# Three-pass products in place of plain ones, a convolution product cut into pieces among attention units, and masks computed one block ahead

## The reference

```python
# block 1: projection, then three mixers whose outputs are joined and projected
cb, cc, cx, nq, nk, nv, gqkv, gz, ga, gb = jnp.split(hmix @ w_in[l], split_at, axis=-1)
y_conv = cb * _dwconv(cc * cx, conv_a_w[l])
y_na   = _neighbourhood_attention(...)          # 4 heads, bias added to the scores
y_gdn  = _gdn_mixer(...)                        # chunked gated delta rule, both directions
# inside it: lower = (kb @ k.T) * dec_strict ; a unit lower triangular solve per chunk of 64
#            intra = (q @ k.T) * dec_incl
...
# then y = concat(y_conv, y_na, y_gdn) @ w_out, and a mixture of 32 experts, 2 of them per token
```

## Time and profile before

| what | value |
|---|---|
| median of 3 runs | 3724.31 us |
| the profiled execution, its own time | 3726.51 us |
| its span from first to last instruction | 3724.6 us |
| PE busy | 3312.6 us, 89% of the span |
| DVE busy | 1811.9 us, 49% |
| ACT busy | 1243.9 us, 33% |
| granted TensorE clock, mean | 0.926 of full |
| share of the chain that ended last | PE 83%, DVE 8%, ACT 4%, issue 3%, DMA 1% |

### The profile page before, as it was taken

How to read it: one execution, slowest core, us unless ns; L and a number is a source line. 1 busy time by engine, 2 the same in 40 slices (tenths; PEclk the granted TensorE clock), 3 DMA queues, 4 the chain that set the end, 5 groups by cost and what they waited for, 6 DMA issues and landing times.

```text
span 3724.6 us, 34562 instructions
## 1 busy us (share of the span) xinstructions
PE 3312.6 (89%) x13568; PEld 2320.0 (62%) x13568; DVE 1811.9 (49%) x2689; ACT 1243.9 (33%) x1864; POOL 44.4 (1%) x76
## 2 busy tenths in 40 slices
PE   7987678789999976899899899999799978969997
PEld 3644676467667653658664378877577755438786
DVE  5335554256566544513562145554598855133343
ACT  2215113255555533215242122222422254032233
POOL 0000000000000000000000000000000000000000
PEclk9998889889999997999899999999899966989999
DMA  8420001379999962212013125541122210103220
GB/s 287 153 96 1 1 1 65 140 293 385 384 379 390 376 252 101 91 68 91 23 46 113 62 76 190 189 151 62 43 79 88 91 68 1 68 23 113 79 79 23
DMA packets 146798, 486.12 MB, mean 131 GB/s; under 512 B 8176, under 2 KB 11888, under 8 KB 134128
## 3 DMA queue, kind: packets, MB, share of 16 engines
q1 hardware_dynamic: 130544, 438.58, 31.6%
q10 hardware_dynamic: 10368, 24.79, 1.7%
q0 software_dynamic: 5760, 20.97, 1.4%
HBM read 459.15 MB, written 25.17 MB: 130 GB/s over the span
## 4 chain that ended last, share of the span: by engine, by line
PE 83%; DVE 8%; ACT 4%; issue 3%; DMA 1%; SPq 0%; POOL 0%; POOLq 0%; ACTq 0%; DVEq 0%; PEldq 0%
PE bank L456 15%; PE bank L458 14%; PE bank L457 14%; PE bank L355 14%; PE bank L1603 5%; PE bank L1114 3%; PE bank L2182 2%; PE bank L553 2%; PE bank L2766 2%; PE bank L545 1%; PE bank L2788 1%; PE bank L1571 1%; DMA ring<-in_w_ada 1%; PE bank L2776 1%; PE bank L2626 0%
## 5 line engine op out<-in xcount | busy, mean ns | idle before, releaser
L457 PE MATMUL bank<-h_parts,A_parts 128*128 128x512 f32 x1424 | 561.3, 394 | 0.0
L355 PE MATMUL bank<-A,ring 128*128 128x512 f32 x800 | 350.0, 600 | 15.1 <-DVE A L1260 8.4
L456 PE MATMUL bank<-h_parts,A_parts 128*128 128x512 f32 x816 | 323.4, 396 | 35.9 <-DVE h_parts L2984 13.4
L458 PE MATMUL bank<-h_parts,ring_parts 128*128 128x512 f32 x848 | 333.8, 394 | 0.0
L445 ACT ACTIVATE A_parts<-ring 128x1024 fp32r<-128x1024 f32 x162 | 170.4, 1053 | 420.9 <-PE bank L458 420.1
L457 PEld LDWEIGHTS bank<-h_parts,A_parts 128*128 128x128 f32 x1424 | 271.7, 191 | 58.6 <-issue 3.8
L452 DVE TENSOR_TENSOR ring_parts<-ring,A_parts 128x1024 fp32r<-128x1024 f32 x162 | 198.0, 1223 | 205.4 <-ACT A_parts L445 205.4
L355 PEld LDWEIGHTS bank<-A,ring 128*128 128x128 f32 x800 | 153.9, 193 | 209.4 <-issue 193.0
L1642 DVE TENSOR_TENSOR ring_parts<-ring,h_parts 128x1024 fp32r<-128x1024 f32 x192 | 225.7, 1221 | 42.7 <-ACT h_parts L1705 41.9
L458 PE MATMUL bank<-h_parts,A_parts 128*128 128x512 f32 x576 | 227.6, 395 | 0.0
L456 PE MATMUL bank<-A_parts 128*128 128x512 f32 x544 | 214.8, 395 | 5.3 <-DVE A_parts L2492 5.2
(11 more groups left out here) (493 smaller groups left out, 5398.5 us busy)
## 6 DMA issues: line engine op xcount, KB each, us to landing
ring<-in_expert_w SPq DMA_DIRECT2D x64, 2048.0 KB, 9.3
ring<-in_w_in SPq DMA_DIRECT2D x37, 2048.0 KB, 7.9
A<-in_expert_w SPq DMA_DIRECT2D x32, 2048.0 KB, 9.4
ring<-in_w_ada SPq DMA_DIRECT2D x24, 2048.0 KB, 12.4
ring<-in_w_ff SPq DMA_DIRECT2D x16, 2048.0 KB, 7.6
slot_rows<-A ACTq DMA_DIRECT2D x32, 512.0 KB, 9.2
ring<-in_w_ffn_gate SPq DMA_DIRECT2D x5, 2048.0 KB, 7.7
ring<-in_w_ffn_up SPq DMA_DIRECT2D x5, 2048.0 KB, 7.9
```

Of the source, the lines that this page charges most:

```text
L355: mm = pe.matmul(bank[tile % 4][:], ring_tile(g)[:, k, m * P:(m + 1) * P], rhs(k), start=(k == 0), stop=(k == g.kt - 1))
L456: pe.matmul(out, parts(w_high), parts(r_low), start=start, stop=False)
L457: pe.matmul(out, parts(w_high), parts(r_high), start=False, stop=False)
L458: return pe.matmul(out, parts(w_low), parts(r_high), start=False, stop=stop)
```

## The change

- Five products go from `project` to `project_split`: `out`, `wa2`, `wb2`, `wo2`, `wo3`. Their activations are parted too: `high_of` (a copy on ACT, 128 by 512) and `low_of` (a subtraction on DVE).
- `co3`, the convolution's output product, also becomes three-pass, and is cut into 32 pieces of two weight squares (6 matmuls) that stand in loops 5 to 22 of the attention: one ahead of `turn(u)`, a second behind it. All pieces write bank 1, so `turn` keeps bank 0 alone. `back` stands one loop later, and so does the DVE step `to_gates` behind it. The sum of the two branches, formerly per tile behind `co3`, is done by column blocks inside the attention and at its end.
- The masks of block b+1 are cut into stages that stand between the steps of block b's inverse. Two constant squares are joined into four, which leaves 9 DVE operations per direction instead of 10.
- `bias_dve` moves ahead into the input projection. Neighbourhood attention no longer waits for `ada11` at its start.
- The bias row in block 2 is added by PE (a matmul of one row per square) instead of DVE.
- Ring slots of block 3: `co3` and `wo3` use slots 0 and 1, the first `ff1` granules slots 2 and 3, whose loads wait for the end of `wo3`. All five first expert loads wait for the end of `out`, formerly two were issued ahead of it.

```diff
@@ in_dve, na_pe
             gdn_decays_dve(dve)
+            bias_dve(dve)
...
-            pe.wait_ge(sem("tile_read"), L["ada11"][0].first_tile + 1)
+            pe.wait_ge(sem("tile_read"), L["xq_in"][0].first_tile + 4)
@@ block1_pe (the same way on ACT and DVE)
+            mask_rows_pe(pe, 0)
+            mask_dots_pe(pe, 0, 0)
+            mask_dots_pe(pe, 0, 1)
             for b in range(TT):
-                gdn_masks_pe(pe, b)
                 for k in range(1, 11):
                     for d in range(2):
                         inverse_pe(pe, b, d, k)
+                    if b + 1 < TT:
+                        if k == 1:
+                            mask_rows_pe(pe, b + 1)
+                        if k in (2, 3):
+                            mask_dots_pe(pe, b + 1, k - 2)
@@ block1_dve
+                    if k >= 2 and b + 1 < TT:
+                        mask_dve(dve, b + 1, k, step)
@@ out_pe (wa2, wb2, wo2 and wo3 likewise)
-            project(pe, L["out"], lambda k: W(MIXED[k]))
+            project_split(pe, out_slices, out_high, mixed_high, lambda k: W(MIXED[k]),
+                          first=lambda k: pe.wait_ge(sem("mixed_split"), k + 1))
@@ gmlp_pe
-                    mm = pe.matmul(bank[4 + g % 2][:, t * P:(t + 1) * P], v_tok(t)[:, g * P:(g + 1) * P], spatial(g),
-                                   start=True, stop=True)
+                    pe.matmul(bank[4 + g % 2][:, c], sq("ones")[0:1, :], head(row2(2), g)[0:1, :], start=True, stop=False)
+                    mm = pe.matmul(bank[4 + g % 2][:, c], v_tok(t)[:, g * P:(g + 1) * P], spatial(g),
+                                   start=False, stop=True)
@@ hg_dve
+            for j in range(HH):
+                dve.wait_ge(sem("y_b_high"), j + 1)
+                low_of(dve, W(24 + j), W(8 + j)).then_inc(sem("y_b_split"), 1)
...
+            for s in wbo_slices[:2]:
+                split_low(dve, s, wbo_high)
@@ hg_act, in the loop over the tiles of gb2
+                act.wait_ge(*seen("y_b", j + 1))
+                high_of(act, W(8 + j), W(24 + j)).then_inc(sem("y_b_high"), 1)
@@ block 3
+        CO_COUNT = [2 if 5 <= u <= 17 or u == 20 else 1 if 18 <= u <= 22 else 0 for u in range(len(dunits))]
+            def co_piece(n):
+                s, k0 = co_slices[n // 4], 2 * (n % 4)
+                tile = s.g.first_tile + s.m
+                if k0 == 0:
+                    pe.wait_ge(sem("split_low"), s.q + 1)
+                    pe.wait_ge(sem("tile_read"), tile)
+                w_high = s.shaped(coo_high(s.q % 2))
+                for k in (k0, k0 + 1):
+                    if n < 4:
+                        pe.wait_ge(sem("conv_split"), k + 1)
+                    mm = three_passes(pe, bank[1][:], w_high[:, k, :], s.raw()[:, k, :], conv_high(k), W(16 + k),
+                                      k == 0, k == KD - 1)
@@ diff_pe
                 if u + 2 < len(dunits):
                     scores(u + 2)
+                if CO_PIECES[u]:
+                    co_piece(CO_PIECES[u][0])
                 turn(u)
+                if CO_PIECES[u][1:]:
+                    co_piece(CO_PIECES[u][1])
+                if u % DIFF_H == 1 and u > 1:
+                    back(u // DIFF_H - 1)
                 if u:
                     mix(u - 1)
-                if u and u % DIFF_H == 0:
-                    back(u // DIFF_H - 1)
@@ out3_pe
-            project(pe, L["co3"], lambda k: W(16 + k))
-            pe.wait_ge(*seen("merged3", KD))
-            project(pe, L["wo3"], W)
+            project_split(pe, wo3_slices, coo_high, lambda k: W(8 + k), W,
+                          first=lambda k: pe.wait_ge(sem("merged3_split"), TT + k // 4))
```

More of the change, by code:

```diff
@@ L213, in plan @@
             slot, places = 0, 2
[L214 to L215 removed]
+        if g is layers["ff1"][0]:
+            slot, places = 2, RING
         loads[slot] += 1
@@ L518, in project_deep_split, with high_of, low_of @@
                 start = ends
+        def high_of(act, dst, src):
+            return act.activation(parts(dst), src, ACT.Copy)
+        def low_of(dve, t, high):
+            return dve.tensor_tensor(parts(t), t, parts(high), ALU.subtract)
         def read_tile(eng, tile, first=False):
@@ L1048, in gdn_masks_pe @@
                 pe.wait_ge(*seen("row_exp", 2 * b))
-            c = slice(b * P, (b + 1) * P)
-            for j in range(GH):
-                pe.matmul(head(bank[0][:], j), W(16 + j)[:, c], W(16 + j)[:, c], start=True, stop=True)
-                pe.matmul(head(bank[1][:], j), W(16 + j)[:, c], W(12 + j)[:, c], start=True, stop=True)
             for d in range(2):
@@ L1854, in block1_act @@
                         inverse_act(act, b, d, k)
+                    if k == 3 and b + 1 < TT:
+                        for d in range(2):
+                            mask_act(act, b + 1, d)
             scan_act(act)
@@ L2114, in build @@
             g.also = seen("hg_summed", HH)
+        wb_slices, wo_slices = tile_slices(*L["wb2"]), tile_slices(*L["wo2"])
+        wbo_slices = wb_slices + wo_slices
+        for i, s in enumerate(wbo_slices):
+            s.before = wbo_slices[i - 2] if i >= 2 else None
+        wbo_high = lambda slot: A[:, 32 + 2 * slot:34 + 2 * slot, :].rearrange("p a n -> p (a n)")
         i_head = lambda b, j: i_tok(b)[:, j * P:(j + 1) * P]
@@ L2612, in build @@
         conv_sq, conv_r = (lambda i: ring[:, 2, (4 + i) * T:(5 + i) * T]), ring[:, 2, 6 * T:7 * T]
-        for g in L["wo3"]:
-            g.also = norm_at("conv_ln", "scaled", KD)
+        co_slices, wo3_slices = tile_slices(*L["co3"]), tile_slices(*L["wo3"])
+        coo_slices = co_slices + wo3_slices
+        for i, s in enumerate(coo_slices):
+            s.before = coo_slices[i - 2] if i >= 2 else None
+        coo_high = lambda slot: ring[:, 2, 2 * T * slot:2 * T * (slot + 1)]
+        conv_high = lambda k: ring[:, 3, k * T:(k + 1) * T]
+        for g in L["ff1"][:2]:
+            g.also = ("tile_ready", L["wo3"][-1].first_tile + 4)
         def in3_pe(pe):
```

293 lines of the change are left out of this document (212 added, 81 removed).

## The result

The changed kernel takes 3623.2 us, the median of 4 runs (3618.6 to 3630.2); the kernel before took 3724.0 us beside it. The ratio is 0.973, 95% interval 0.9713 to 0.9746. On another chip the same kernel took 3618.5 us (four runs, 3614.7 to 3622.2), ratio 0.9707 (0.9691 to 0.9723). The prediction was 3574 us with a range of 3545 to 3645: the sign and the range hold, the point was 49 us too low. The time also lies outside the 3550 to 3600 us for which the 0.70 of the forecast itself was given.

What follows compares the result with a forecast made beforehand. PE work plus short stretches where PE waits for dependent steps was taken as the bound; terms -10, -42, -13.5, -8.7, -21, -45 and -10.5 summed to -150.7 us from 3726.5, giving 3574 us after a 2.2 us median correction, range 3545 to 3645.

Steps and rivals of the forecast that it cites:

- the 0.70 of the forecast itself: Whole kernel: chance given to the forecast of 3574 us, with 3550 to 3600 us as its own range.
- an attention that stays at half clock: Rival, last attention: pieces do not raise PE's clock, +24 us instead of -45, 3643 us; chance 0.13.
- One rival: Slower than before: passes stay at half clock in all six three-pass products, +111 us, given as 3685 us; chance 0.03.
- The joined products: Three-pass products: 192 passes, 43.5 us each, instead of plain products of 55 to 57 us; `out` -13.5 us.
- The masks: Delta rule: masks between the steps save 12.5 us per transition, three times, and 4 us in the first block: -42 us.
- my bounds: Delta rule masks: -30 to -50 us, the latter if idle stretches no longer cost PE its clock.
- Block 2: Spatial mixing 18 us, +4.7, with bias on PE; `wa2` in three passes -13.4; together -8.7 us.
- the upper bound of the spatial stage: Block 2's spatial mixing: +12 us if PE's clock stays cold throughout; the lower bound was +1.
- The last attention: Attention with `co3`'s pieces: full clock from the second loop with pieces, 168 us instead of 213.3: -45 us.
- DVE is the bound: Rival, delta rule and last attention: masks save 25 instead of 42, attention 30 instead of 45, 3606 us; chance 0.10.
- Neighbourhood attention: Its start: bias table moved into the input projection, first score sum at about 263.1 instead of 271.88: -10 us.
- `wb2` and `wo2`: Two three-pass products: `wb2` -8 us after a 3.4 us wait for its first slice, `wo2` -13; together -21 us.

Runs made afterwards that it cites:

- the kernel with DVE's bias: Against the changed kernel, block 2's spatial mixing bias is added by DVE again instead of by PE's single-row multiplications: 3579.1 us, ratio 0.9603.
- the 128-row experiment: Against the changed kernel, block 2's bias multiplications on PE use all 128 rows (identity times bias) instead of one row: 3589.0 us, ratio 0.9624.
- The order experiment: Against the changed kernel, DVE reads a finished tile ahead of norming the rows, and PE's second piece stands behind the turning back: 3613.3 us, ratio 0.9697.

## Why the prediction came out as it did

**The number.** The range held for a reason that I had not given. Its upper end, 3645 us, was there for an attention that stays at half clock; what brought the time to 3623 us was block 2, 31 us off, and the attention, 14.5 us off though at full clock. Masks that won 5 us more than forecast hid some of it, and the profiled execution lost another 9 us in the neighbourhood attention. One rival was added up wrongly: +111 us on the kernel before is 3835 us, where I wrote 3685, which would not have been slower at all.

**The joined products were right.** `out` -13.3 (predicted -13.5), `wo3` -10 (-10.5), `wa2` -12.9 by the kernel with DVE's bias (65.8 against 78.7 us), the two of block 3 27.2 together. 192 passes at 0.227 us replace the plain product, and no tile but the first of a product waited for its parts.

**The masks were right in kind and 5 us too small.** The period came out at 31.5 us for my 33 to 35. In DVE's timeline step 6 is this row, and steps 10 are the two shown above.

```profile
408.84 1.41 DVE L1163 TENSOR_TENSOR ring<-ring,bank 128x512 f32<-128x512 f32 x2
```

So step 6 starts 20.2 us behind step 10, where I had 21, and the last four steps take 11.3 us for my 11.6; on top of that I had taken 1.2 us off each transition for waits that the count turned out to hold already. That the idle stretches no longer cost PE its clock (0.95 instead of 0.82 over the whole stretch) was in my bounds and not in my sum.

**Block 2 is the step that failed.** I wrote that "at half clock a group of 8 records costs 5.72 / 4 = 1.43 us and 16 would cost 2.9", and took two cold groups and six warm ones. The price per record was read from 128-row multiplications that follow one another, and misread: those 5.72 us hold both levels of the clock.

```profile
1574.00:1576.00 2.00, 2.00 (x11) 2.00 (x11) 1.23 (x2) 0.00 (x0) 0.00 (x0) 0.50 0.00 0
1576.00:1578.00 2.00, 2.00 (x17) 2.00 (x17) 1.74 (x4) 0.00 (x0) 0.00 (x0) 0.90 0.00 0
```

At half clock a record takes 0.21 us (a multiplication of two starts every 0.43 us in the timeline of the 128-row experiment) and 16 of them 3.4. A single-row multiplication between two of 128 rows has yet another price: at half clock the 16 records cost 5.8 us. And the groups never became warm, where those of before were warm from their third on. I had given +12 as the upper bound of the spatial stage; it came out at +33. Of the 21 us between, the misread price explains 4. Block 2 is 31 of the 54 us by which the profiled sum was missed.

**The last attention was forecast at 168 us from first scores to `wo3` and took 182.8.** The mechanism was right: full clock from the first loops with pieces. Up to unit 8 it took 32.7 us (I had 35), and the loops of row block 1 4.9 us (4.7 to 5.2). Missing were two things: at the row blocks' ends, which I had put at a flat 5 us each, the tile read stood behind the norming in DVE's queue, and behind the end of row block 2 the clock fell, so that three loops took 6.2 to 6.5 us instead of 3.4. The order experiment brings 9.5 to 9.9 us of the 14.8 back. My rival "DVE is the bound" is what comes next: it sets the pace of row block 3 as soon as PE is fast there.

**Neighbourhood attention** was priced at -10; ten of twelve profiles show -6 to -11, 8 in the mean, and the profiled execution of the changed kernel did not show it. Nothing in my working said that the clock's rise there is a matter of chance.

**`wb2` and `wo2`**: the wait of 3.16 us was forecast (3.4); the half clock behind it, 2.9 us in this profile, was not.

The rule of the Trainium skill that I weighed ("TensorE: Matmul & The Clock Gate", section "What's actually happening": activity releases the throttle) has to be read by what the rows show here. With single rows between full ones a PE busy for 46 us did not release it; the same stage with 128 rows did after 3.5 us. In the attention of the kernel before, with its 64-row scores and no pieces, the clock stayed at 0.50 for some 130 us, also where PE was full, and rose only in row block 3; with three-pass pieces it rose some 22 us in. By busy time alone the two kinds cannot be told apart.

The same page of the Trainium skill says in its section "The mechanism" that a weight load overlaps a running multiplication only when the row groups differ. If a load of one row and one of 128 count as differing, the alternation should have helped or done nothing by that. The rows disagree: with equal rows the multiplications stand 0.43 us apart, with alternating rows 0.72 us, at one clock. But the one row is also among the 128, and whether that counts as differing no run here shows.

## What to carry to other kernels

Price a multiplication by rows of its own shape and in its own company: a sliver of one row put among full ones cost more than the vector operation that it replaced, and the identity with all rows, or the vector engine, did the same work 32 to 35 us cheaper. Full-row work put into a stretch of small multiplications can be paid for in large part by the clock that it holds up and the waits that it fills (22 of 36 us here); look at what becomes of the stretch behind the last piece, and at what stands ahead of the short operations in the other engines' queues. And take more than one profile of a stretch that starts at half clock before you say what an edit there is worth.

## What the runs showed of the hardware

- Float32 multiplications of 128 columns at a granted clock of 0.50: 0.43 us each (two records) when all have 128 rows, 0.72 us when they alternate with single-row ones, with load and multiplication starting together.
- The granted clock of a full PE stayed at 0.50 for 46 us in that alternation, and rose 3.5 us into the same stage with 128 rows.
- In the neighbourhood attention the clock rose early or after 25 us, under the same instructions in different executions, up to 10 us of the stage's time; a wait of 3.16 us ahead of `wb2` was followed by 14 slow passes in seven profiles, by 8 in one and by none in four.
